# Second norm's scale and shift rows spread by GpSimd broadcasts in place of TensorE products with ones

## The reference

```python
for i in range(DEPTH):
    ...
    y = jnp.concatenate([h_loc, h_mem], axis=-1) @ w_out[i]
    x = layer_norm(ALPHA * x + y, ln1_g[i], ln1_b[i])
    m = grouped_moe(x.reshape(nb * seq, d), router_w, router_b,
                    w_gate[i], w_up[i], w_down[i]).reshape(nb, seq, d)
    x = layer_norm(ALPHA * x + m, ln2_g[i], ln2_b[i])
```

## Time and profile before

| | |
|---|---|
| median of 3 runs | 1393.65 us |
| lowest, highest | 1392.25, 1394.54 us |
| the profiled execution, span | 1392.8 us |
| TensorE busy | 1338.4 us, 96% |
| VectorE busy | 509.8 us, 37% |
| ScalarE busy | 306.1 us, 22% |
| GpSimd busy | 41.4 us, 3% |
| read from HBM | 460.05 MB |

### The profile page before, as it was taken

One profiled execution on the slowest core, in us unless ns is written; L12 is line 12 of the kernel. 1 busy time (PEld: TensorE's weight loads), 2 busy tenths in 40 slices (PEclk: granted clock), 3 DMA queues, 4 the chain that ended last, 5 costly groups with the idle time before them and its releaser, 6 DMA issues. The chain is left out here.

```text
span 1392.8 us, 16438 instructions
## 1 busy us (share of the span) xinstructions
PE 1338.4 (96%) x6694; PEld 711.7 (51%) x6694; DVE 509.8 (37%) x1038; ACT 306.1 (22%) x534; POOL 41.4 (3%) x66
## 2 busy tenths in 40 slices
PE   8999999999999999989899999999999999999896
PEld 7878783333333333333787788774333333333332
DVE  5366583122122121222554358782132122122122
ACT  5242341011011010111443236441011011010111
POOL 1000000000000000000000000000000000000000
PEclk9999999999999999999999999999999999999998
DMA  9420879999999999999431201989999999999995
GB/s 376 172 92 0 363 293 372 427 426 428 427 425 427 427 428 426 427 428 392 190 121 61 106 16 61 409 335 382 429 428 426 428 426 428 428 425 428 427 427 225
DMA packets 41395, 465.36 MB, mean 334 GB/s; under 512 B 6602, under 2 KB 6754, under 8 KB 13030
## 3 DMA queue, kind: packets, MB, share of 16 engines
q1 hardware_dynamic: 36422, 454.83, 78.4%
q0 software_dynamic: 4608, 8.40, 1.6%
q10 hardware_dynamic: 288, 1.05, 0.2%
HBM read 460.05 MB, written 12.60 MB: 339 GB/s over the span
## 5 line engine op out<-in xcount | busy, mean ns | idle before, releaser
L1244 PE MATMUL bank<-ring,kv_sb 128*64 128x512 f32 x960 | 214.7, 596 | 11.2 <-DMA ring<-in_w_pack 11.1
L1244 PE MATMUL bank<-ring,onehot 128*64 128x512 f32 x896 | 203.7, 603 | 13.4 <-DMA ring<-in_w_pack 13.4
L1294 PE MATMUL bank<-ring,pad 128*64 128x512 f32 x928 | 211.8, 598 | 1.8 <-issue 1.1
L1244 PEld LDWEIGHTS bank<-ring,kv_sb 128*64 128x64 f32 x960 | 68.4, 137 | 135.8 <-issue 135.5
L1294 PEld LDWEIGHTS bank<-ring,pad 128*64 128x64 f32 x928 | 61.8, 136 | 143.8 <-issue 135.0
L1244 PEld LDWEIGHTS bank<-ring,onehot 128*64 128x64 f32 x896 | 64.4, 138 | 131.7 <-issue 131.7
L1407 ACT ACTIVATE pad<-bank 128x256 f32<-128x256 f32 x64 | 24.5, 383 | 437.1 <-PE bank L1244 437.1
L1413 ACT COPY pad<-bank 128x512 f32<-128x512 f32 x64 | 37.4, 585 | 329.2 <-PE bank L1294 329.2
L1497 DVE COPY onehot<-bank 128x512 f32<-128x512 f32 x32 | 22.1, 691 | 237.0 <-PE bank L1230 237.0
L1507 DVE COPY pad<-bank 128x256 f32<-128x256 f32 x64 | 27.0, 422 | 173.5 <-PE bank L1269 173.5
L1497 DVE COPY kv_sb<-bank 128x512 f32<-128x512 f32 x28 | 19.4, 691 | 188.8 <-PE bank L1230 188.8
(11 more groups left out here) (345 smaller groups left out, 1723.4 us busy)
## 6 DMA issues: line engine op xcount, KB each, us to landing
ring<-in_w_pack SPq DMA_DIRECT2D x166, 2048.0 KB, 27.3
xT<-in_w_pack SPq DMA_DIRECT2D x18, 2048.0 KB, 30.1
ring<-in_w_pack SPq DMA_DIRECT2D x16, 1024.0 KB, 25.1
ring<-in_mlstm_w_in SPq DMA_DIRECT2D x6, 2048.0 KB, 8.4
ring<-in_conv_slabs SPq DMA_DIRECT2D x5, 1536.0 KB, 12.1
ring<-in_w_out SPq DMA_DIRECT2D x1, 4096.0 KB, 13.8
x_rows<-x_sb SPq DMA_DIRECT2D x6, 512.0 KB, 8.2
ring<-in_xT SPq DMA_DIRECT2D x4, 512.0 KB, 6.7
```

The costliest lines, as they stand in the source:

```text
L1244: last = nc.tensor.matmul(GU_BANK[e % 2][64 * f:64 * f + 64, :], xgT[e // 2 % 2][:, 4 * h + c, 64 * (e % 2):64 * (e % 2) + 64], gu[:, c, f ...
L1294: last = nc.tensor.matmul(Y_BANK[e % 2][64 * n:64 * n + 64, :], hidT[e % 2][:, c, 64 * f:64 * f + 64], dn[:, f, c, 512 * n:512 * n + 512], ...
```

## The change

The four `spread_ln` products of TensorE, the four `ln_in` copies of ScalarE, the semaphore between them and the banks set aside for them go. GpSimd spreads each row from partition 0 over all 128 partitions of the same tile with one `partition_broadcast` of 1024 columns, after waiting for the two loads and ahead of its wait for the tokens' numbers. VectorE's first `finish` waits for the two broadcasts.

```diff
-                ln_spread, ln_copied = s("p2_ln_spread"), s("p2_ln_copied")
+                ln_spread = s("p2_ln_spread")
...
-                LN_BANK = (bank[7], bank[5])
...
                         if l == 0:
                             conv_pool(pool)
+                        pool.wait_ge(in_ln, 32)
+                        for rows in (ln_g, ln_b):
+                            nc.gpsimd.partition_broadcast(rows[:, :], rows[0:1, :]).then_inc(ln_spread, 1)
                         pool.wait_ge(indexed, 1)
                         pool.wait_ge(stored, 16 * TT)
                         pool.wait_ge(xturned, 2)
...
-                        def spread_ln(i):
-
-                            row, n = (ln_g, ln_b)[i // 2], i % 2
-                            pe.wait_ge(in_ln, 32)
-                            if i >= 2:
-                                pe.wait_ge(ln_copied, i - 1)
-                            nc.tensor.matmul(LN_BANK[n][:, :], ones_f[0:1, :], row[0:1, 512 * n:512 * n + 512],
-                                             start=True, stop=True).then_inc(ln_spread, 1)
...
                                 turn_hidden(0)
-                                spread_ln(0)
-                                spread_ln(1)
                                 down(0)
                                 turn_rows(2)
-                                spread_ln(2)
                             turn_rows(e + 2)
-                            if e == 2:
-                                pe.wait_ge(ln_copied, 4)
...
                                 turn_gates(e // 2)
-                            if e == 1:
-                                spread_ln(3)
                             turn_hidden(e)
...
-                        def ln_in(i, dst):
-                            for n in range(2):
-                                act.wait_ge(ln_spread, 2 * i + n + 1)
-                                nc.scalar.copy(dst[:, 512 * n:512 * n + 512], LN_BANK[n][:, :]).then_inc(ln_copied, 1)
-
                         for e in range(N_EXPERTS):
                             activate(e)
-                            if e == 1:
-                                ln_in(0, ln_g)
                             if e:
                                 put_out(e - 1)
-                            if e == 1:
-                                ln_in(1, ln_b)
...
                             if g == 0:
-                                dve.wait_ge(ln_copied, 4)
+                                dve.wait_ge(ln_spread, 2)
```

## The result

The changed kernel takes 1399.18 us (median of 6 runs, 1396.43 to 1400.82), the kernel before beside it 1393.85 (1392.25 to 1395.09). The ratio is 1.0035 with a 95% interval of 1.0021 to 1.0048: 5.3 us slower, where I had forecast 1394.3, a range of 1390.5 to 1398.5 and no measurable change. The profiled execution took 1398.84 us, its span is 1396.8, 4.0 more than that of before.

A forecast was written before the change was run, and what follows sets the result against it. The expert stages' weight stream was taken to bound the kernel. Terms: -0.3 us for TensorE, +1.0 for VectorE's delay in two layers, 0 for the rest, +0.7 in all on 1393.65: 1394.3 us, range 1390.5 to 1398.5.

The forecast's parts named there:

- The row without operands: GpSimd, ahead of the broadcasts: loads their code in idle time, cost 0, upper end 0.4 us.
- The products: TensorE, before `gate_up(2)`: removing four products per layer gains about 0.13 us a layer, VectorE's chain covering the rest.
- Broadcasts beside VectorE: VectorE's two-input products before `code_rows`: broadcasts delay TensorE 0.5 us a layer; rival of full-length blocking 1398.0, chance 0.10.
- the 0.94 of slack: VectorE's slack in us between its last two-input product and the last quarter of `code_rows`, with a 0.26 handover.
- the 0.75 per us of overlap: VectorE's loss beside GpSimd, from L2106 beside a select: 0.435 us for 0.58 us; 1.8 us for two broadcasts.
- The broadcast's duration: GpSimd, per layer two broadcasts of 128x1024: 1.2 us each, with 1.15 and 1.64 as ends.
- their slack: Gathers behind the broadcasts: 6.6 us of slack, exceeded only if broadcasts take 5.9 us each or more.
- The clock: TensorE, half clock from 235.5 to 238.9 us: the same fall expected without the products, at no cost.
- a fall inside `down(0)`: Rival: without the first two products TensorE idles 1.7 us and the clock falls for `down(0)`: +3.1, 1396.8 us, chance 0.06.
- my three signs of being wrong: Broadcasts ending after 222 us, `code_rows` more than 1.5 us late, or TensorE at half clock in `down(0)`.

The follow-up runs named there:

- the kernel with the first repair: Changed kernel plus an 8-element GpSimd iota behind the first three gathers of layer 1: 1393.05 us, ratio 0.9989 to the kernel before.
- the kernel with the tripled broadcasts: Changed kernel plus the iota behind layer 1's gathers, with each broadcast done three times, six in place of two per layer: 1392.98 us, ratio 0.9981.
- the kernel with the code alone: Kernel before, products and copies kept, plus an unread 8-element broadcast behind the first three gathers of layer 1: 1401.50 us, ratio 1.0048.
- the repaired kernel with products put back: Changed kernel plus the iota behind layer 1's gathers, with the four TensorE products per layer restored, results unread, no ScalarE copies: 1393.29 us.
- The repaired kernels without products: Changed kernel with iota behind layer 1's gathers 1393.05 us, memsets before first select 1392.10, broadcasts behind gathers plus iota 1392.38 and 1392.32, tripled broadcasts 1392.98.
- the small broadcast and the iota behind it: Kernel before plus an unread 8-element broadcast behind layer 1's first gathers: 1401.50 us; with an 8-element iota right behind that broadcast: 1393.89 us.
- the silent end: Changed kernel with the 8-element iota behind the last scatter of layer 1, at the program's end: 1398.37 us, ratio 1.0027.

## Why the prediction was wrong, by its steps

- **The row without operands: the step that failed.** I costed the code load in front of the broadcasts "at 0", with 0.4 us from its bytes as the upper end, because GpSimd is idle around it. For that load this held: it is about 9 us long and hidden, as when the broadcasts stood behind the gathers and GpSimd idled 8.80 us ahead of them in layer 0 without cost. I did not ask what the other row of the same kind, at the program's start, would do once the code it wants is no longer in place. It costs 8.8 to 9.2 us there, 7.0 of the time when alone (1401.50 against 1394.54). The bytes were no bound: the instruction queue of the earlier trace rows moves 0.18 MB in both programs. The Trainium skill has the mechanism that I passed over: "GPSIMD Engine Reference", section "2.1 Instruction dispatch", says that the first call into freshly loaded code pays for a load with no visible instruction, about 6 us. The trace agrees on the invisible gap; the price here is 6.96 us with hardly anything beside it and 8.8 to 12.2 beside other transfers, and the measurement decides.
- **The products: mis-sized.** I had 0.13 us a layer, they cost 0.53 in the layer measured. I took the 0.26 us between VectorE's copy and the second `turn_rows` for TensorE's handover. Where TensorE is idle the handover is 0.05 us: in the kernel with the first repair the copy ends at 232.92 and the product starts at 232.97. In before it was the third product itself, 232.20 + 1.12 = 233.32, that held the second `turn_rows` at 233.25, a modelled end overlapping the next start; and the fourth held `turn_hidden(1)` likewise. The small overlap was in the rows; I read the copy as releaser because no idle time was printed.
- **Broadcasts beside VectorE: right in kind, 0 in effect.** I took 0.5 us a layer. One of four comparisons fell beside a broadcast in layer 0 and none in layer 1; it took 0.85 us more, less than the 0.94 of slack that I had worked out (1.15 with the handover of 0.05), and four more broadcasts a layer cost nothing that the times show. By the full block of the Trainium skill ("SBUF — State Buffer", "Who interferes with whom") the comparison would have waited for the end of the first broadcast: in the kernel with the tripled broadcasts from 211.25 to 212.38, 1.13 us. The trace agrees that the one that comes later pays, the comparison or the broadcast; what it pays, 0.85 us, is less than a full block, and is the 0.75 per us of overlap that I took.
- **The broadcast's duration: right.** 2.46 us for both in layer 1, 1.2 each predicted. The gathers had their slack; the rows had landed by 218.0, 6.9 us behind SP's issue, where I had 6.2.
- **The clock.** I said the fall would not depend on the products, and gave 0.06 to a fall inside `down(0)`. It did lie there in the profiled execution, but it does so with the products too: `down(0)` took 5.19 us in the kernel with the code alone. So one of my three signs of being wrong came true and says less than I gave it. Where the fall lies changes from execution to execution: the second profiled execution of the changed kernel had none in `down(0)` or `gate_up(2)` of either layer, and in the repaired kernel with products put back layer 0 had none. Over the thirteen profiled executions a fall lies on one of these two in 6 of 8 layers with the products and in 6 of 18 without: that it is the same with and without them is not shown.

The measured parts: +7.0 for the load at the start and -2 x 0.53 for the products give +5.9; measured +5.3 (interval +2.9 to +6.7). The 1.7 us between the layers would make it +4.2, near the 4.0 by which the spans of the two profiled executions differ. The repaired kernels without products lie 1.5 to 2.7 us below the kernel before, of which the products explain 1.1. The shorter idle time between the layers can be the rest: the kernel with products put back has no copies and yet the long one, 16.53 us, which speaks against ScalarE's copies. But that kernel's time, 0.24 above the first repaired one, does not show it, and the cause stays open.

## What to carry to other kernels

Ask of every new kind of GpSimd instruction which code it needs and what the program leaves in place at its end, for the bill comes at the start of the next execution, far from the edit. Where two codes are needed, bring the first one back while GpSimd waits for others, or put what the other engines need first ahead of the load. And look at the first microseconds of a program in the plan of a change too, even if the diff is elsewhere.

## What the runs showed of the hardware that was not expected

- A code load is a gap behind a row of some 10 ns: 8.77 to 9.21 us at the start, 8.80 to 9.32 for the broadcasts' code, 10.05 to 12.19 us for the first code beside the weight stream and 6.96 at the silent end.
- The code in place outlasts an execution, as the small broadcast and the iota behind it show.
- A broadcast of one row of 1024 f32 to 128 partitions takes 1.3 us, two in a row 2.46. When a VectorE comparison with two inputs has begun before it, it takes 2.2 to 2.3; when the broadcast began first, it keeps its time and the comparison takes 2.06 us instead of 1.21.
- The granted clock of an execution goes with its time, by and large: of 34 runs of the kernel before, the four with a mean of 0.997 took 1393.2 us on average, the fifteen with 0.995 took 1395.1, the four with 0.994 took 1396.3.
